# A hybrid encoder layer on one core: the head rebuilt (norm weights turned by TensorE, x split straight from PSUM, sums of squares per token, first two weight tiles worked on alternately)

## The chip, the core and the metric

The kernel runs on one core of a Trainium2 chip. The time is device microseconds for one execution; before the change the median of three runs is 1083.7 us (1081.27 to 1084.81). The engines are TensorE (PE, matmuls; its weight loads are PEld), VectorE (DVE), ScalarE (ACT), GpSimd (POOL) and SyncE (SP), which here only issues DMAs.

## The reference

One encoder layer on x of shape 1 x 512 x 1024 in float32:

```python
x = x + 0.5 * swiglu(rmsnorm(x, ffn1_norm), ffn1_w_gate, ffn1_w_up, ffn1_w_down)
h = rmsnorm(x, mix_norm); p = h @ w_in
# p -> differential attention (4 heads, relative bias) and Hyena (FFT convolution)
x = x + concat([att_out, hy_out]) @ w_out
x = x + 0.5 * swiglu(rmsnorm(x, ffn2_norm), ffn2_w_gate, ffn2_w_up, ffn2_w_down)
return rmsnorm(x, final_norm)

def rmsnorm(x, g): return x * rsqrt(mean(x * x, axis=-1) + 1e-6) * g
def swiglu(x, wg, wu, wd): return (silu(x @ wg) * (x @ wu)) @ wd
```

D_FF is 2816. The Hyena filters come from a small network of three layers on positions (33 -> 64 -> 64 -> 64, with sines), which reads only its own inputs.

## The kernel before

The activations lie transposed: eight blocks of 128 features by 512 tokens. `resid` holds x, `x_hi` and `x_lo` are the two halves (high and low part, fp32r) of x times the norm's gain, and 1/rms of each token is multiplied on afterwards (`rinv`, 128 x 512). A weight tile is 1024 x 128 numbers (512 KB). SP loads it into one of four slots of `raw`, ScalarE rounds it to `w_hi` (`split`, two buffers), VectorE subtracts to get `w_lo`, and TensorE does 24 matmuls of 128 x 512 in the routine `tile` (three for each of eight blocks: hi x hi, hi x lo, lo x hi; L1079 to L1081). The tiles have numbers in the order in which they are used, n0 to n167; the first half-step `gate_up` takes n0 to n43, four for each of 11 iterations (gate, up, gate, up).

Each engine has its own program, written out by hand, and they meet only at semaphores. SP issues in program order: the four chunks of x (L343), n0 to n3, then `others()` (25 small and middle loads, among them the four 512 KB tables `cos_t`, `sin_t`, `cos_i`, `sin_i`), and then n4 and so on. The raw slot of n4 is that of n0.

The head: TensorE turns x (`x_nat`, tokens on partitions) block by block through four PSUM banks (L1126); VectorE copies each block to `resid` (L783), ScalarE squares it (L453) and makes `x_hi` (L455), GpSimd adds the squares into `ssq` (L383), VectorE makes `x_lo` (L698). TensorE sums `ssq` over the partitions after n0 (L1090), ScalarE takes the root, VectorE inverts 128 x 512 (L703). The gain comes by a DMA that puts 1024 single numbers into columns.

The filter network's three matmuls (`mlp`, L1117) are in the iterations 0, 1 and 2 of `gate_up`, between its second and third tile; VectorE forms the sine's argument (`mlp_argument`, L715 and on) between the scaling of gate (L744) and up (L749). A matmul `vec` follows iteration 2.

Of the kernel before, what the change touches and what calls it, by code (L numbers as in the profile page):

```python
# [8 lines left out]
F32 = mybir.dt.float32  # L31
# [39 lines left out]
X_BANKS = (3, 4, 5, 6)  # L71
# [24 lines left out]
def build(nc, a, out):  # L96
    ctx = ExitStack()
    with ctx:
# [32 lines left out]
        soft, _ = place("soft", [P, 8])  # L131
        mlp_c, _ = place("mlp_c", [FO, 4])
# [46 lines left out]
        spec_q, _ = place("spec_q", [P, NT, S], at=attn_t_at)      # L179
# [7 lines left out]
        x_nat, _ = place("x_nat", [P, NT, D], at=hid_at)  # L187

# [34 lines left out]

        x_turned, resid_set, resid_sq, ssq_added, x_hi_made, x_split = (
# [58 lines left out]
        def _(sp):  # L283
# [36 lines left out]
            def gate_up(wg, wu, n_first):  # L320
# [7 lines left out]
                body(0)  # L328
                if n_first == N_FF1:
                    others()  # L330
                with sp.Fori(1, NF // 2) as i:
                    body(i)
# [9 lines left out]
            for k in range(4):  # L342
                sp.dma_start(x_nat[:, :, 2 * k * P:2 * (k + 1) * P], x[:, :, 2 * k * P:2 * (k + 1) * P]).then_inc(x_landed[k], 16)  # L343
            gate_up(a["ffn1_w_gate"][0], a["ffn1_w_up"][0], N_FF1)
# [20 lines left out]
        def _(pool):  # L365
# [9 lines left out]
            def squares(s):  # L375

                wait(pool, ssq_summed, s)
                nc.gpsimd.memset(ssq[:], 0.0).then_inc(ssq_added, 1)
                with pool.Fori(0, KD // 2) as i:
                    for b in range(2):  # L380
                        pool.wait_ge(resid_sq, number(KD * s + b + 1, 2, i))
                        pool.wait_ge(ssq_added, number((KD + 1) * s + b + 1, 2, i))
                        nc.gpsimd.tensor_tensor(ssq[:], ssq[:], sq[:, b, :], ALU.add).then_inc(ssq_added, 1)  # L383

            squares(0)

# [47 lines left out]
        def _(act):  # L434

            act.dma_start(ident[:], a["c_ident"]).then_inc(ident_landed, 16)
            with nc.allow_non_contiguous_dma(reason="columns of constants"):
                act.dma_start(cols[:, COLS["ffn1_norm"]:COLS["ffn1_norm"] + KD],
                              a["ffn1_norm"].rearrange("o (k p) -> p (o k)", p=P)).then_inc(gain_landed, 16)
# [9 lines left out]
            def resid_block(s, j, stride=0, i=0):  # L449
                at = number(j, stride, i)  # L450
                act.wait_ge(resid_set, number(KD * s + j + 1, stride, i))
                wait(act, ssq_added, number((KD + 1) * s + j, stride, i))
# [5 lines left out]
            def root(s):  # L458

                act.wait_ge(ssq_summed, s + 1)  # L460
# [7 lines left out]
            def gate_up(ffn, n_first, i, first=False, other=None):  # L468
                for b in range(2):
# [3 lines left out]
                    if not (first and b == 1):  # L473
# [3 lines left out]
                    if early:  # L477
# [5 lines left out]
                    split(8, n + (3 if early else 2), 4, i)  # L483
# [10 lines left out]

            act.wait_ge(consts_set, 4)
            act.wait_ge(gain_landed, 16)
# [958 lines left out]
```

## Time and profile before

| | |
|---|---|
| median of three runs | 1083.7 us |
| span of the profiled execution (first to last instruction) | 1079.7 us |
| time around the span (median less span) | 4.0 us |
| TensorE busy | 1042.6 us, 97% |
| VectorE busy | 576.0 us, 53% |
| ScalarE busy | 335.2 us, 31% |
| first weight matmul starts | 18.82 us |
| tile n4 starts | 46.68 us |
| mean granted TensorE clock | 0.990 |

TensorE is the engine to read: the others are busy half the time or less. A busy share near 1 says that what comes out of a faster head is kept only where TensorE isn't made to wait afterwards.

### The profile page before, as it was taken

How to read it: one execution, taken by the hardware profiler on the slowest of the kernel's cores; microseconds unless marked ns; L12 is line 12 of the kernel's file. 1: busy time of each engine (PE TensorE's matmuls, PEld its weight loads, DVE VectorE, ACT ScalarE, POOL GpSimd, SP SyncE). 2: the span in 40 equal slices, each digit the busy share in tenths (PEclk: the TensorE clock that was granted, in tenths of full speed). 3: DMA queues.
4: the chain of work that ended last, by engine and by line, in shares of the span. 5: the costliest groups of instructions: out<-in, count | busy, mean ns of one | idle time of the engine just before them, and what ended most of it. 6: DMA issues, size and time to landing. Idle time of an engine off the chain costs nothing. (4 is left out here: it accounts for less than half of the span.)

```text
span 1079.7 us, 12092 instructions
## 1 busy us (share of the span) xinstructions
PE 1042.6 (97%) x4524; PEld 818.8 (76%) x4524; DVE 576.0 (53%) x722; ACT 335.2 (31%) x475; POOL 72.4 (7%) x65
## 2 busy tenths in 40 slices
PE   5999999999999999999999969999999999999996
PEld 4776888888888875777775558778888888888885
DVE  5755545444333348876958495764444444433332
ACT  4322222222222232444444303442222323222222
POOL 4000000000000010000000070310000000000000
PEclk9999999999999999999999989999999999999999
DMA  8622333333323252323211000233333333323322
GB/s 165 197 85 80 96 97 97 97 97 92 98 83 107 88 168 81 95 59 96 78 59 59 1 20 20 78 99 97 97 97 97 97 97 93 96 88 93 91 66 78
DMA packets 185483, 96.67 MB, mean 90 GB/s; under 512 B 15843, under 2 KB 182883, under 8 KB 185448
## 3 DMA queue, kind: packets, MB, share of 16 engines
q1 hardware_dynamic: 183160, 92.70, 29.6%
q10 hardware_dynamic: 1936, 1.64, 0.5%
q0 software_dynamic: 352, 1.85, 0.5%
q8 instruction: 23, 0.38, 0.2%
q14 instruction: 12, 0.10, 0.0%
HBM read 94.07 MB, written 2.11 MB: 89 GB/s over the span
## 5 line engine op out<-in xcount | busy, mean ns | idle before, releaser
L1079 PE MATMUL bank<-x_hi,w_hi 128*128 128x512 f32 x896 | 355.3, 397 | 3.8 <-DVE w_lo L677 2.1
L1080 PE MATMUL bank<-x_lo,w_hi 128*128 128x512 f32 x896 | 349.7, 390 | 0.0
L1081 PE MATMUL bank<-x_hi,w_lo 128*128 128x512 f32 x896 | 349.6, 390 | 0.0
L677 DVE TENSOR_TENSOR w_lo<-raw,w_hi 128x1024 fp32r<-128x1024 f32 x168 | 204.6, 1218 | 225.6 <-ACT w_hi L446 219.9
L446 ACT CAST w_hi<-raw 128x1024 fp32r<-128x1024 f32 x168 | 172.2, 1025 | 166.6 <-PE bank L1081 132.5
L1079 PEld LDWEIGHTS bank<-x_hi,w_hi 128*128 128x128 f32 x896 | 168.7, 188 | 50.5 <-issue 8.6
L1080 PEld LDWEIGHTS bank<-x_lo,w_hi 128*128 128x128 f32 x896 | 168.9, 188 | 35.7 <-issue 1.4
L1081 PEld LDWEIGHTS bank<-x_hi,w_lo 128*128 128x128 f32 x896 | 168.8, 188 | 35.4
L1081 PE MATMUL bank<-h_hi,w_lo 128*128 128x512 f32 x352 | 138.7, 394 | 0.0
L1079 PE MATMUL bank<-h_hi,w_hi 128*128 128x512 f32 x352 | 138.7, 394 | 0.0
L1080 PE MATMUL bank<-h_lo,w_hi 128*128 128x512 f32 x352 | 138.7, 394 | 0.0
L383 POOL TENSOR_TENSOR ssq<-ssq,sq 128x512 f32<-128x512 f32 x32 | 43.9, 1371 | 693.9 <-ACT sq L453 693.3
L485 ACT CAST h_hi<-bank 128x512 f32 (+1 forms) x44 | 25.8, 587 | 207.7 <-DVE bank L754 207.7
L1079 PEld LDWEIGHTS bank<-h_hi,w_hi 128*128 128x128 f32 x352 | 65.8, 187 | 16.4
L1080 PEld LDWEIGHTS bank<-h_lo,w_hi 128*128 128x128 f32 x352 | 65.8, 187 | 16.3
L1081 PEld LDWEIGHTS bank<-h_hi,w_lo 128*128 128x128 f32 x352 | 65.8, 187 | 16.2
L749 DVE TENSOR_TENSOR bank<-bank,rinv 128x512 f32<-128x512 f32 x44 | 30.8, 699 | 70.5 <-PE bank L1081 70.3
L482 ACT ACTIVATE silu<-bank 128x512 f32<-128x512 f32 x44 | 26.4, 599 | 133.7 <-DVE bank L744 133.7
L744 DVE TENSOR_TENSOR bank<-bank,rinv 128x512 f32<-128x512 f32 x44 | 30.8, 699 | 39.5 <-PE bank L1081 39.4
L757 DVE TENSOR_TENSOR h_lo<-bank,h_hi 128x512 f32 (+1 forms) x44 | 30.4, 691 | 36.5 <-ACT h_hi L485 36.5
L453 ACT ACTIVATE sq<-resid 128x512 f32<-128x512 f32 (+1 forms) x32 | 20.1, 629 | 85.1 <-DVE resid L692 69.2
L698 DVE SCALAR_TENSOR_TENSOR x_lo<-resid,cols,x_hi 128x512 fp32r<-128x512 f32 (+1 forms) x24 | 31.2, 1313 | 17.8 <-ACT x_hi L455 17.7
(185 smaller groups left out, 750.2 us busy)
## 6 DMA issues: line engine op xcount, KB each, us to landing
raw<-in_ffn_w_gate SPq DMA_DIRECT2D x44, 512.0 KB, 3.8
raw<-in_ffn_w_up SPq DMA_DIRECT2D x44, 512.0 KB, 3.8
raw<-in_ffn_w_down SPq DMA_DIRECT2D x32, 512.0 KB, 3.5
raw<-in_w_in SPq DMA_DIRECT2D x24, 512.0 KB, 3.7
raw<-in_ffn_w_down SPq DMA_DIRECT2D x16, 384.0 KB, 3.1
raw<-in_w_out SPq DMA_DIRECT2D x8, 512.0 KB, 3.5
x_nat<-in_x SPq DMA_DIRECT2D x4, 512.0 KB, 6.2
out<-o_nat SPq DMA_DIRECT2D x8, 256.0 KB, 2.9
```

The lines of the kernel that those rows point to most:

```text
L383: nc.gpsimd.tensor_tensor(ssq[:], ssq[:], sq[:, b, :], ALU.add).then_inc(ssq_added, 1)
L446: nc.scalar.copy(w_hi[:, half, 0:kb, :], raw[:, slot, 0:kb, :]).then_inc(w_hi_made, 1)
L482: nc.scalar.activation(silu[:, b, :], bank[b][:], ACT.Silu).then_inc(gate_act, 1)
L485: nc.scalar.copy(h_hi[:, number(b, 2, i), :], bank[2 + b][:]).then_inc(h_hi_made, 1)
L677: nc.vector.tensor_tensor(w_lo[:, half, 0:kb, :], raw[:, slot, 0:kb, :], w_hi[:, half, 0:kb, :].bitcast(F32), ALU.subtract).then_inc(w_spl ...
L698: nc.vector.scalar_tensor_tensor(x_lo[:, at, :], resid[:, at, :], cols[:, bass.ds(at + COLS[GAIN[s]], 1)], x_hi[:, at, :].bitcast(F32), AL ...
L744: nc.vector.tensor_tensor(bank[b][:], bank[b][:], rinv[:], ALU.mult).then_inc(gate_scaled, 1)
L749: nc.vector.tensor_tensor(bank[2 + b][:], bank[2 + b][:], rinv[:], ALU.mult).then_inc(up_scaled, 1)
L757: nc.vector.tensor_tensor(h_lo[:, at, :], bank[2 + b][:], h_hi[:, at, :].bitcast(F32), ALU.subtract).then_inc(h_split, 1)
L1079: nc.tensor.matmul(dst, w_hi[:, half, k, :], hi, start=first and k == 0, stop=False)
L1080: nc.tensor.matmul(dst, w_hi[:, half, k, :], lo, start=False, stop=False)
L1081: ins = nc.tensor.matmul(dst, w_lo[:, half, k, :], hi, start=False, stop=last and k == kb - 1)
```

## The change

- SP issues n0 first, then two chunks of x, n1, two chunks of x, n2 and n3; `others()` stays ahead of n4.
- The norm's gain is loaded as eight rows of 128 and turned by a TensorE transpose; VectorE copies it to `cols`.
- TensorE begins with ten matmuls on the constant `ones`. The turned blocks of x go to six banks; `x_hi` and `x_lo` are made from the bank, with the gain. `resid` is copied beside that (two blocks by ScalarE, six by VectorE).
- n0 and n1 are worked on in pieces (`x_part`), between the turning of the chunks.
- The sum of squares comes from ScalarE, per token, on `x_nat` (four activations of 128 x 1024 with an accumulated output), the root and the reciprocal are 128 x 4, and four matmuls in the middle of n2 spread it over `bank[7]`. GpSimd has no part in it.
- The root table is loaded at the start. The iteration 0 has no `mlp`: the network's steps are in iterations 1, 2, 3.
- In the rest the counts of the semaphores are lowered by what the head no longer does; the work is the same.

The core of the diff:

```diff
+                    load(g[:, :, 0:P], KD, 0)
+                    x_chunk(0)
+                    x_chunk(1)
+                    load(u[:, :, 0:P], KD, 1)
+                    x_chunk(2)
+                    x_chunk(3)
+                    load(g[:, :, P:2 * P], KD, 2)
+                    load(u[:, :, P:2 * P], KD, 3)
                     others()
...
+            act.dma_start(gain_rows[:], a["ffn1_norm"].rearrange("o (k p) -> (o k) p", p=P)).then_inc(gain_landed, 16)
...
-            squares(0)
...
+            nc.scalar.activation(x_r[:, 12:13], eps[:], ACT.Sqrt)
+            split(8, 0)
+            act.wait_ge(gain_set, 1)
+            x_high(0)
+            x_high(1)
+            split(8, 1)
+            x_high(2)
+            x_keep(0)
+            x_high(3)
+            x_keep(1)
+            for j in range(4, KD):
+                x_high(j)
...
+            for i in range(5):
+                gate_up(0, N_FF1, i, first=i == 0, other=(lambda: mlp_sin(i - 2)) if i > 1 else None)
...
+            split(8, 0)
+            x_low(0)
+            x_low(1)
+            split(8, 1)
+            for j in range(2, KD):
+                x_low(j)
+            for j in range(KEPT_BY_ACT, KD):
+                nc.vector.tensor_copy(resid[:, j, :], bank[X_BANKS[j]][:]).then_inc(x_kept, 1)
+            for i in range(4):
+                gate_up(0, N_FF1, i, first=i == 0, other=mlp_argument(i - 1) if i else ())
...
+                    if first and ffn == 0:
+                        if b == 0:
+                            continue
+                        pe.wait_ge(x_kept, 2)
+                        tile(bank[1][:], x_ops, 2, between=x_spreads)
+                        pe.wait_ge(x_kept, 3)
+                        tile(bank[3][:], x_ops, 3)
+                        continue
...
+            for _ in range(WARM):
+                nc.tensor.matmul(bank[0][:, 0:P], ones[:], ones[:], start=True, stop=True)
             pe.wait_ge(ident_landed, 16)
...
+            x_turn(0)
+            x_turn(1)
+            pe.wait_ge(w_split, 1)
+            x_part(0, (0, 1))
+            x_turn(2)
+            pe.wait_ge(w_split, 2)
+            x_part(1, (0, 1))
+            x_part(0, (2, 3))
+            x_turn(3)
+            x_part(0, (4, 5, 6, 7))
+            x_part(1, (2, 3, 4, 5, 6, 7))
+            for i in range(4):
+                gate_up(0, N_FF1, i, first=i == 0, other=(lambda: mlp(i - 1)) if i else None)
```

SP's program from its start, before (`raw` is a tile's load, w_gate and w_up by turns, so n0 to n3):

```order
L343 DMA x_nat<-in_x 128x4x256 x4
L290 DMA raw<-in_ffn_w_gate 128x8x128
L290 DMA raw<-in_ffn_w_up 128x8x128
L290 DMA raw<-in_ffn_w_gate 128x8x128
L290 DMA raw<-in_ffn_w_up 128x8x128
L294 DMA z_t<-in_c_z 33x512
```

And in the change:

```order
L275 DMA raw<-in_ffn_w_gate 128x8x128
L338 DMA x_nat<-in_x 128x4x256 x2
L275 DMA raw<-in_ffn_w_up 128x8x128
L338 DMA x_nat<-in_x 128x4x256 x2
L275 DMA raw<-in_ffn_w_gate 128x8x128
L275 DMA raw<-in_ffn_w_up 128x8x128
L279 DMA z_t<-in_c_z 33x512
```

The tiles n0 and n1 moved between the chunks of x; what follows them, z_t and the rest of `others()`, starts at the same place.

TensorE's program around the network's first matmul, before (between n1 and n2):

```order
L1079 MATMUL bank<-x_hi,w_hi 128x512
L1080 MATMUL bank<-x_lo,w_hi 128x512
L1081 MATMUL bank<-x_hi,w_lo 128x512
L1117 MATMUL bank<-z_t,w_115 64x512 [waits mlp_landed]
L1079 MATMUL bank<-x_hi,w_hi 128x512 [waits w_split]
```

And in the change (between n5 and n6):

```order
L1130 MATMUL bank<-x_hi,w_hi 128x512
L1131 MATMUL bank<-x_lo,w_hi 128x512
L1132 MATMUL bank<-x_hi,w_lo 128x512
L1178 MATMUL bank<-z_t,w_117 64x512 [waits mlp_landed]
L1130 MATMUL bank<-x_hi,w_hi 128x512 [waits w_split,h_split]
```

The matmul on `z_t` is the same; it stands four tiles later, behind n4 and n5.

## Rows read from the trace of the kernel before

**Rows 1.** The page: span, and busy time (share) and instructions of TensorE

```profile
span 1079.7 us, 12092 instructions
...
PE 1042.6 (97%) x4524; PEld 818.8 (76%) x4524; DVE 576.0 (53%) x722; ACT 335.2 (31%) x475; POOL 72.4 (7%) x65
```

**Rows 2.** Waits of TensorE, whole span, the first: us in total, times, longest us

```profile
PE bank L1313 <- DVE spec_p L1028: 8.9, 2, 8.7
```

**Rows 3.** Timeline of SP's queue: start us, us, what it issued

```profile
10.29 1.72 SPq L290 DMA_DIRECT2D raw<-in_ffn_w_up  x1
12.05 1.28 SPq L294 DMA_DIRECT2D z_t<-in_c_z  x1
...
30.69 0.48 SPq L290 DMA_DIRECT2D raw<-in_ffn_w_gate  x1
```

**Rows 4.** DMA issues, us to landing: x (min/median/max), n3's and n4's

```profile
DMA to landing us min/median/max: 4.1/6.2/8.1
...
raw<-in_ffn_w_up SPq DMA_DIRECT2D x1, 512.0 KB, 7.3
...
raw<-in_ffn_w_gate SPq DMA_DIRECT2D x1, 512.0 KB, 10.4
```

**Rows 5.** Timeline of TensorE: first transposes, n0's matmuls; chain of work: last transposes

```profile
5.03 3.65 PE L1126 MATMUL bank<-ident,x_nat 128*128 128x128 f32 x16 [5.03 <-DMA x_nat<-in_x]
...
22.38 0.63 PE L1081 MATMUL bank<-x_hi,w_lo 128*128 128x512 f32 x1
22.81 0.63 PE L1079 MATMUL bank<-x_hi,w_hi 128*128 128x512 f32 x1
...
1067.08 3.28 PE bank L1392 x28
```

**Rows 6.** Timelines of all engines: a split into its matmul, and n4's

```profile
27.28 1.21 DVE L677 TENSOR_TENSOR w_lo<-raw,w_hi 128x1024 fp32r<-128x1024 f32 x1
...
28.64 0.19 PEld L1079 LDWEIGHTS bank<-x_hi,w_hi 128*128 128x128 f32 x1 [0.24 <-DVE w_lo L677]
...
41.24 0.39 PE L1079 MATMUL bank<-x_hi,w_hi 128*128 128x512 f32 x1
...
43.42 1.04 ACT L446 CAST w_hi<-raw 128x1024 fp32r<-128x1024 f32 x1
...
44.49 1.23 DVE L677 TENSOR_TENSOR w_lo<-raw,w_hi 128x1024 fp32r<-128x1024 f32 x1 [1.60 <-ACT w_hi L446]
...
46.68 0.39 PE L1079 MATMUL bank<-x_hi,w_hi 128*128 128x512 f32 x1
```

**Rows 7.** Timeline of TensorE around mlp(0), and at n7 and n11

```profile
34.33 0.39 PE L1081 MATMUL bank<-x_hi,w_lo 128*128 128x512 f32 x1
...
35.65 0.50 PE L1079 MATMUL bank<-x_hi,w_hi 128*128 128x512 f32 x1
...
65.67 0.50 PE L1079 MATMUL bank<-x_hi,w_hi 128*128 128x512 f32 x1 [1.27 <-DVE w_lo L677]
...
88.62 0.39 PE L1081 MATMUL bank<-x_hi,w_lo 128*128 128x512 f32 x1
89.86 0.50 PE L1079 MATMUL bank<-x_hi,w_hi 128*128 128x512 f32 x1 [0.85 <-DVE w_lo L677]
```

**Rows 8.** Stretches (busy of each engine, granted clock, DMA share, GB/s) and timeline

```profile
627.00:636.00 9.00, 0.31 (x3) 0.06 (x1) 8.86 (x8) 1.04 (x1) 8.86 (x7) 0.72 0.00 0
636.00:641.00 5.00, 5.00 (x12) 4.01 (x13) 4.96 (x8) 0.00 (x0) 0.35 (x1) 0.50 0.07 3
...
635.94 6.32 PE L1313 MATMUL bank<-cos_i,spec_p 128*128 128x256 f32 x16 [8.69 <-DVE spec_p L1028]
647.71 3.61 PE L1313 MATMUL bank<-sin_i,spec_q 128*128 128x256 f32 x16
```

**Rows 9.** Groups by line and form, 0 to 60 us: busy, mean ns of one

```profile
L698 DVE SCALAR_TENSOR_TENSOR x_lo<-resid,cols,x_hi 128x512 fp32r<-128x512 f32 x8 | 9.2, 1150 | 2.6 <-ACT x_hi L455 2.4
...
L744 DVE TENSOR_TENSOR bank<-bank,rinv 128x512 f32<-128x512 f32 x3 | 2.1, 699 | 1.0 <-PE bank L1081 0.9
```

More of the change, by code:

```diff
@@ L472, in gate_up @@
                     early = first and b == 0
-                    if not (first and b == 1):
+                    head = early and ffn == 0
+                    if not (first and b == 1) and not head:
                         split(8, n + 1, 4, i)
@@ L482, in gate_up @@
                     nc.scalar.activation(silu[:, b, :], bank[b][:], ACT.Silu).then_inc(gate_act, 1)
[L483 removed]
+                    if not head:
+                        split(8, n + (3 if early else 2), 4, i)
                     act.wait_ge(h_made, number(f0 + 1, 2, i))
@@ L737, in gate_up @@
                     early = first and b == 0
-                    if not (first and b == 1):
+                    head = early and ffn == 0
+                    if not (first and b == 1) and not head:
                         split(8, n + 1, 4, i)
-                    if early:
+                    if head:
+                        split(8, 2)
+                        x_inverse()
+                        split(8, 3)
+                        x_rinv()
+                    elif early:
                         split(8, n + 2, 4, i)
@@ L749, in gate_up @@
                     nc.vector.tensor_tensor(bank[2 + b][:], bank[2 + b][:], rinv[:], ALU.mult).then_inc(up_scaled, 1)
-                    if early:
+                    if early and not head:
                         split(8, n + 3, 4, i)
@@ L1070, in _, with tile @@
         def _(pe):
-            def tile(dst, operand, n0, stride=0, i=0, first=True, last=True, ready=None):
+            def tile(dst, operand, n0, stride=0, i=0, first=True, last=True, ready=None, between=None):
                 half = n0 % SPLIT
@@ L1128, in _, with x_turn @@
-            pe.wait_ge(consts_set, 4)
-            for i in range(3):
-                gate_up(0, N_FF1, i, first=i == 0, other=lambda: mlp(i))
+            def x_turn(k):
+                pe.wait_ge(x_landed[k], 16)
+                for j in (2 * k, 2 * k + 1):
+                    if j >= 6:
+                        pe.wait_ge(x_kept_act, j - 5)
+                        pe.wait_ge(x_split, j - 5)
+                    for t in range(NT):
+                        ins = nc.tensor.transpose(bank[X_BANKS[j]][:, t * P:(t + 1) * P], x_nat[:, t, j * P:(j + 1) * P], ident[:])
+                    ins.then_inc(x_turned, 1)
@@ new lines, in x_part @@
+            def x_part(n, ks):
+                for k in ks:
+                    pe.wait_ge(x_split, k + 1)
+                    hi, lo = x_ops[k]
+                    nc.tensor.matmul(bank[2 * n][:], w_hi[:, n, k, :], hi, start=k == 0, stop=False)
+                    nc.tensor.matmul(bank[2 * n][:], w_hi[:, n, k, :], lo, start=False, stop=False)
+                    ins = nc.tensor.matmul(bank[2 * n][:], w_lo[:, n, k, :], hi, start=False, stop=k == KD - 1)
+                if ks[-1] == KD - 1:
+                    ins.then_inc(w_used, 1)
@@ new lines, in x_spreads @@
+            def x_spreads():
+                pe.wait_ge(x_inv, 1)
+                pe.wait_ge(x_kept, 4)
+                for t in range(NT):
+                    ins = nc.tensor.matmul(bank[7][:, t * P:(t + 1) * P], x_r[:, 8 + t:9 + t].to_broadcast([P, P]), ident[:],
+                                           start=True, stop=True)
+                ins.then_inc(x_spread, 1)
+            pe.wait_ge(consts_set, 1)
+            for _ in range(WARM):
+                nc.tensor.matmul(bank[0][:, 0:P], ones[:], ones[:], start=True, stop=True)
```

122 lines of the change are left out of this document (72 added, 50 removed).

## The prediction

> **What bounds the kernel now.** I read the page's share of busy time first, then the waits of TensorE, then the timelines of the first 50 us and the single DMA issues. TensorE is busy 97% of the span [rows 1]. Of its waits over the whole execution [rows 2] the largest is 8.9 us before the inverse transform, which the change doesn't touch; at the head it waits for x until 5.03 [rows 5] and then within the turning of x. From the first weight tile on, TensorE runs tile after tile: 24 matmuls of 512 columns, from 41.24 to 46.68, are 5.44 us [rows 6], 0.227 us each. So whatever the head wins is kept only if TensorE is fed without a pause up to the point where both kernels do the same again. The tiles are numbered n0, n1, ... in the order of their weights. n0 to n3 have their raw slots free from the start; n4 is the first whose load stands in SP's program behind the small loads of `others()`, in both kernels. I take **the start of tile n4** as the common point: 46.68 us before [rows 6].
>
> SP issues the last early tile (n3) at 10.29, begins `others()` at 12.05, which ends with the tables `cos_t`, `sin_t`, `cos_i`, `sin_i` (512 KB each), and issues n4's load only at 30.69 [rows 3]. That load lands 10.4 us later [rows 4], at 41.1, since 2 MB of tables are ahead of it in the same queue. ScalarE rounds it at 43.42, VectorE makes the low part at 44.49 [rows 6]. Before, n4 thus landed 2.3 us before it was rounded: the load was covered, but barely.
>
> **The change, part by part.**
>
> *The head on TensorE, if nothing else limited it.* The DMA order becomes n0, x chunks 0 and 1, n1, x chunks 2 and 3, n2, n3. Before, x landed from 4.9 us on, chunk 3 at 10.5 (4.1 and 8.1 us after issues at 0.75 and 2.4), n3 at 17.6 [rows 3, 4]: 7.1 us for four tiles of weights, 1.8 each, and at the rate of the first chunks 1.5 to 1.8 for one of x. Laid out anew: n0 5.3, x0 6.9, x1 8.4, n1 10.3, x2 11.8, x3 13.3, n2 15.1, n3 16.9. Sixteen transposes take 3.65 us at the start and 28 take 3.28 us at the end of the kernel [rows 5]. Turning chunks 0 and 1 fills 6.9 to 10.6 at the slower pace. Then come 48 matmuls of n0 and n1 and 16 transposes: 48 x 0.227 + 16 x 0.117 = 12.8 us, and some 0.6 us for what still runs at the low clock: n1 ends near 24.0. ScalarE and VectorE keep up. Their steps are about 0.7 us for each block (a multiply on VectorE out of a bank and `rinv` has mean 0.70 [rows 9]), and the two squares on either side of n2's rounding stand behind no matmul: 1.2 us each, a little over the 1.04 us of a rounding of 1024 elements [rows 6]. The six copies of x to `resid` on VectorE (0.61 us apart) end at 22.6, n2's low part at 23.8, just before it is wanted. n2 and n3 take 10.9 us, the spreading of 1/rms 0.9 (four fp32 matmuls on 128 columns: between four passes of 0.117 and eight of 0.228, so 0.5 to 1.8). **TensorE finishes n3 near 35.8**, 10.9 us before it did. Taken off the path on the way: eight squares and additions (ScalarE, GpSimd), a root table load, a reciprocal of 128x512. I price them at nothing by themselves, since their gain is in the 35.8. The ten matmuls on `ones` and the turning of the norm's rows stand before x lands (20 passes of 0.228 are 4.6 us, from 1 us on), and cost nothing. `x_lo` is now made from a bank: 0.70 by the nearest bank operand, 1.15 by its own mean beside a busy GpSimd [rows 9]; eight times the difference is 3.6 us and would put n3's end at 39.4. Should the clock rise only at 15.6 instead of about 12, n3 ends at 37.6; with the low clock until 23 us, as before, at some 41.3. The start of n4 below doesn't depend on it.
>
> *What n4 waits for.* n4's load still follows `others()`. The gains of the head move SP only through its back-pressure: the issue of n3 took until 12.0 as I read it because the queue was full [rows 3]. With the column load of `ffn1_norm` (1024 elements of 4 bytes) gone and n0's packets first, I put the end of that issue at 11.0, and z_t's, held 1.3 us before, 0.5 to 1 us earlier than it was. From there to 30.69 SP is paced by its own issues, 0.4 to 0.6 us each, which are the same. So n4 lands 0 to 1.3 us earlier; I take 0.8: 40.3. From landing to the first matmul: 0.15 for the hop (x landed at 4.85, the first transpose began at 5.03 [rows 5]), 1.08 from rounding to the low part, 1.21 to its end and 0.15 to the weight load (27.28 + 1.21 = 28.49, load at 28.64) [rows 6]. Sum 2.6: **n4 starts at 42.9**, against 46.68: 3.8 us won, and TensorE stands idle for 7.1 us, from 35.8 on. Of the 10.9 us, 7.1 are lost there.
>
> *The filter network moves by one iteration.* `mlp(0)` ran on TensorE in iteration 0, ahead of n4; now it follows n5. Its price there: from the start of the last matmul, 34.33, to the next tile's first, 35.65, is 1.32 instead of 0.23, so 1.09 us [rows 7]. That is owed after n4, and is subtracted. Besides, each of the iterations 1 and 2 before has a wait for `w_lo` at its fourth tile, since VectorE's up-scaling stands behind the wait for the network's matmul, then `h`, `h_hi` and ScalarE's next rounding behind it: idle 1.27 at 65.67 and 0.85 at 89.86 [rows 7], with the lost pace 1.4 and 1.0 us (88.62 to 89.86 is 1.24 instead of 0.23). Iteration 0 had none; now iterations 1, 2 and 3 have one each. One more: 1.0 to 1.4, I take 1.2.
>
> *The clock after the idle stretch.* The one long pause before, 8.7 us up to 635.94, shows what follows: over 627 to 636 the granted clock averages 0.72, so it fell from 2.4 to 1.2 GHz within the pause; over 636 to 641 it is 0.50, and 16 matmuls took 6.32 us that later took 3.61 [rows 8]: 2.7 us. Pauses of 1.3 us and less cost nothing of the kind [rows 7]. Bounds 0 and 2.7; at 7.1 us I take 2.7, since that is nearer to 8.7 than to 1.3.
>
> The Trainium skill (TensorE: Matmul & The Clock Gate, section HAM oscillation — how this bites in real kernels) speaks against this change in the same way: matmuls that wait for DMA come back at half rate, and the cost of getting the clock back is paid at each such wait. By the rule the 2.7 us stand; if only the short pauses were a guide, the sum would be 2.7 us lower.
>
> *Sum*, against the profiled execution, whose span is 1079.7 [rows 1] and which with 4.0 us around it stands at the median of 1083.7: -3.8 (n4's start) + 1.1 (`mlp(0)`) + 1.2 (one more wait) + 2.7 (clock) = **+1.2 us: 1084.9**. What comes after (projections, attention, transforms, second half) has the same instructions in the same order, and is not moved against itself. GpSimd's additions at the head went alongside VectorE and are gone; nobody on the path feels it after n4.
>
> **The rivals.**
>
> *A: as summed*, 1084.9. Own range 1083.5 to 1086.5 (landing 0 to 1.3, wait 1.0 to 1.4, clock price 2.0 to 2.7).
>
> *B: n4 waits, but the clock stays at 2.4 GHz.* If the head is slower than 35.8 (late clock, late x), the pause gets short while n4's start stays at 42.9; the pauses of 1.3 us left it up [rows 7]. 1083.7 - 1.5 = 1082.2. For: several estimates in the head lean to the optimistic side. Against: it needs 3 us more.
>
> *C: faster, since the pause is much shorter than I make it.* If SP got through `others()` some 2.7 us earlier (DMA queue freer, small issues at 0.43 us throughout instead of 0.6), n4 would start at 41.0 and with the clock up the gain is 3.3 us, the point from which it counts. Were n4's load not held up at all, n4 would start with the end of n3 and the result would be 10.8 - 2.3 = 8.5 us faster, 1075.2. Against: n4's 10.4 us from issue to landing [rows 4] and the unchanged list in front of it.
>
> The Trainium skill (DMA: Bandwidth & Descriptors, section Anatomy of one DMA — SWDGE (gpsimd) path) gives a DMA a fixed 2.0 us and then its bytes at 436 GB/s; for n4's 512 KB that is an estimate of 3.2 us, which would mean this case in full, but the formula has no queue in it, and the 10.4 us measured decide against it.
>
> *D: slower.* The low clock lasts through the whole of n4, not through some 5 us of it: 24 matmuls at 0.43 (22.38 to 22.81 [rows 5]) instead of 0.227 are 4.9 us instead of 2.7, giving 1087.1. It decides from a price of 4.8 us. For: the low stretch of 18.8 to 23.2 and that of 636 were each about 5 us. Against: just that; none lasted 10.
>
> That the two first tiles aren't really alternated, or that the head is slower than before, changes nothing as long as n3 ends before 42.9.
>
> **How the numbers follow.** A 0.50, B 0.25, C 0.13, D 0.12. A measurement of this kernel can tell about 0.3% (3.3 us) from no change. A and B are within it, C is faster, D slower by more than it: but A's and B's edges and the spread of the runs (1081.3 to 1084.8) can carry a little over. Faster 0.14, same 0.75, slower 0.11. The range takes in A and B with that spread and reaches into C and D: 1080.6 to 1087.3.
>
> **What would show it right or wrong.** Right: TensorE's first weight matmul before 12 us, n3's last near 36; then a pause of 5 to 8 us that ends with `w_lo` of n4, SP's issue of n4 still near 30 us, its landing about 10 us later; a granted clock near 0.5 in the 5 us behind the pause; three waits for `w_lo` of 0.8 to 1.3 us in iterations 1, 2, 3. Wrong: n4's load landing before 38 (C); n3 ending after 39 (B); or a difference from the kernel before that arises after the first 110 us, which no step here accounts for.

## The result, and the profile after

The changed kernel takes 1074.21 us (median of 5 runs, 1071.75 to 1077.74), the kernel before in the same comparison 1083.15 us (5 runs, 1078.41 to 1084.81). The ratio on record is 0.994 (it is not the quotient of the two medians, which would be 0.992), with a 95% interval of 0.9912 to 0.9967: faster by 3.6 to 9.5 us. The forecast was 1084.9, with a range of 1080.6 to 1087.3, so it missed on both counts: the time lies below the range, and "same" had 0.75 of the chance.

The page of the changed kernel, its span and the busy times, to be read beside [rows 1]:

```profile
span 1075.9 us, 12082 instructions
...
PE 1040.3 (97%) x4551; PEld 824.4 (77%) x4551; DVE 568.8 (53%) x722; ACT 335.0 (31%) x477; POOL 60.9 (6%) x57
```

Its profiled execution took 1077.74 us, the slowest of its five. The span is 3.8 us shorter than before. The waits of TensorE, the first two (us in total, times, longest us), beside [rows 2]:

```profile
PE bank L1130 <- DVE w_lo L707: 12.0, 5, 9.0
PE bank L1410 <- DVE spec_p L1079: 9.2, 2, 8.7
```

A new wait for `w_lo` of 9.0 us has come in: the pause ahead of tile n4. TensorE's timeline at the head (start us, us, what it did, in brackets the idle time before and what ended it), with ScalarE's and VectorE's step for n4 in between:

```profile
10.07 0.48 PE L1195 MATMUL bank<-x_hi,w_hi 128*128 128x512 f32 x1
...
23.17 0.39 PE L1130 MATMUL bank<-x_hi,w_hi 128*128 128x512 f32 x1
...
34.30 0.39 PE L1130 MATMUL bank<-x_hi,w_hi 128*128 128x512 f32 x1
...
41.70 1.04 ACT L440 CAST w_hi<-raw 128x1024 fp32r<-128x1024 f32 x1 [8.62 <-DMA raw<-in_ffn_w_gate]
42.77 1.22 DVE L707 TENSOR_TENSOR w_lo<-raw,w_hi 128x1024 fp32r<-128x1024 f32 x1 [10.33 <-ACT w_hi L440]
44.14 0.76 PE L1130 MATMUL bank<-x_hi,w_hi 128*128 128x512 f32 x1 [9.00 <-DVE w_lo L707]
```

The first weight matmul runs at 10.07, n2 starts at 23.17, n3 is through at 34.98 (three matmuls after 34.30), and n4, which before started at 46.68 [rows 6], starts at 44.14. SP's queue and the landing of n4, beside [rows 3, 4]:

```profile
10.19 2.82 SPq L279 DMA_DIRECT2D z_t<-in_c_z  x1
...
19.08 2.56 SPq L290 DMA_DIRECT2D cols<-in_hy_bias  x1
...
32.26 0.62 SPq L275 DMA_DIRECT2D raw<-in_ffn_w_gate  x1
```

```profile
raw<-in_ffn_w_gate SPq DMA_DIRECT2D x1, 512.0 KB, 9.4
```

n4 is issued at 32.26 and lands 9.4 us later, at 41.7. What the pause does to the clock shows in three stretches (busy time of TensorE, its weight loads, VectorE, ScalarE and GpSimd, then the granted clock, the DMA share and GB/s):

```profile
34.50:44.00 9.50, 0.64 (x3) 0.19 (x1) 1.23 (x2) 1.04 (x1) 0.00 (x0) 0.64 1.14 333
44.00:47.40 3.40, 3.26 (x8) 2.61 (x9) 2.39 (x4) 1.53 (x2) 0.00 (x0) 0.50 1.15 287
47.40:60.00 12.60, 12.60 (x54) 9.48 (x53) 4.68 (x6) 1.53 (x2) 0.00 (x0) 1.00 0.31 89
```

The clock fell within the pause from 2.4 to 1.2 GHz (mean 0.64), stayed there for the 3.40 us after it, and was back at 1.00.

**Where the two traces part.** A good clock along the kernel is the start of each tile's `w_lo` on VectorE, since all 168 tiles have one. The starts for n20, n44 and n68, first before, then after:

```profile
138.04 1.23 DVE L677 TENSOR_TENSOR w_lo<-raw,w_hi 128x1024 fp32r<-128x1024 f32 x1 [1.60 <-ACT w_hi L446]
268.60 1.23 DVE L677 TENSOR_TENSOR w_lo<-raw,w_hi 128x1024 fp32r<-128x1024 f32 x1 [1.60 <-ACT w_hi L446]
391.82 1.23 DVE L677 TENSOR_TENSOR w_lo<-raw,w_hi 128x1024 fp32r<-128x1024 f32 x1 [4.85 <-ACT w_hi L446]
```

```profile
139.27 1.23 DVE L707 TENSOR_TENSOR w_lo<-raw,w_hi 128x1024 fp32r<-128x1024 f32 x1 [1.60 <-ACT w_hi L440]
269.83 1.23 DVE L707 TENSOR_TENSOR w_lo<-raw,w_hi 128x1024 fp32r<-128x1024 f32 x1 [1.60 <-ACT w_hi L440]
389.65 1.23 DVE L707 TENSOR_TENSOR w_lo<-raw,w_hi 128x1024 fp32r<-128x1024 f32 x1 [4.69 <-ACT w_hi L440]
```

At n20, behind the head and all that it disturbs, the changed kernel is 1.23 us *behind*. At n44 it is still exactly 1.23 behind: the gate and up tiles run at one pace in both. From n44 to n68, the down projection of the first feed-forward block, it gains 3.40 us (+1.23 to -2.17), and in the same stage of the second block (n144 at 939.86, n167 at 1054.01, against 940.07 and 1057.45) another 3.23. The head, which the change is about, gave nothing; stages whose instructions the change doesn't touch gave the time.

### The profile page after: what moved, and what is told of

Its sections match the earlier page's. It is cut to its first block and busy times, and to the rows that moved or that the text cites. A ratio compares the mean times of both kernels' runs of the same rounds, so it can differ in the third digit from the quotient of the medians.

```text
span 1075.9 us, 12082 instructions
## 1 busy us (share of the span) xinstructions
PE 1040.3 (97%) x4551; PEld 824.4 (77%) x4551; DVE 568.8 (53%) x722; ACT 335.0 (31%) x477; POOL 60.9 (6%) x57
## 5 line engine op out<-in xcount | busy, mean ns | idle before, releaser
L1130 PE MATMUL bank<-x_hi,w_hi 128*128 128x512 f32 x880 | 349.4, 397 | 12.4 <-DVE w_lo L707 12.0
L1131 PE MATMUL bank<-x_lo,w_hi 128*128 128x512 f32 x880 | 344.1, 391 | 0.0
L1132 PE MATMUL bank<-x_hi,w_lo 128*128 128x512 f32 x880 | 344.1, 391 | 0.0
L1130 PEld LDWEIGHTS bank<-x_hi,w_hi 128*128 128x128 f32 x880 | 166.2, 189 | 59.9 <-issue 18.8
L1132 PEld LDWEIGHTS bank<-x_hi,w_lo 128*128 128x128 f32 x880 | 166.1, 189 | 35.3
L1131 PEld LDWEIGHTS bank<-x_lo,w_hi 128*128 128x128 f32 x880 | 166.4, 189 | 34.5 <-issue 1.0
L380 POOL TENSOR_TENSOR ssq<-ssq,sq 128x512 f32<-128x512 f32 x24 | 32.5, 1353 | 651.1 <-ACT sq L447 650.8
L447 ACT ACTIVATE sq<-resid 128x512 f32<-128x512 f32 (+1 forms) x24 | 15.1, 630 | 78.2 <-DVE resid L722 67.0
L804 DVE TENSOR_TENSOR bank<-bank,silu 128x512 f32<-128x512 f32 x44 | 30.8, 700 | 4.5
```

The lines of the kernel that those rows point to most:

```text
L804: nc.vector.tensor_tensor(bank[2 + b][:], bank[2 + b][:], silu[:, b, :], ALU.mult).then_inc(h_made, 1)
L1130: nc.tensor.matmul(dst, w_hi[:, half, k, :], hi, start=first and k == 0, stop=False)
L1131: nc.tensor.matmul(dst, w_hi[:, half, k, :], lo, start=False, stop=False)
L1132: ins = nc.tensor.matmul(dst, w_lo[:, half, k, :], hi, start=False, stop=last and k == kb - 1)
```

## The experiments

**Reading the pace of the matmuls.** In the down projection the moving operand is `h_hi` or `h_lo` instead of `x_hi` or `x_lo`; everything else is as in the gate and up tiles. Four starts of TensorE in a row, before and then after:

```profile
330.34 0.39 PE L1079 MATMUL bank<-h_hi,w_hi 128*128 128x512 f32 x1
330.58 0.39 PE L1080 MATMUL bank<-h_lo,w_hi 128*128 128x512 f32 x1
330.81 0.39 PE L1081 MATMUL bank<-h_hi,w_lo 128*128 128x512 f32 x1
331.04 0.39 PE L1079 MATMUL bank<-h_hi,w_hi 128*128 128x512 f32 x1
```

```profile
330.57 0.39 PE L1130 MATMUL bank<-h_hi,w_hi 128*128 128x512 f32 x1
330.80 0.39 PE L1131 MATMUL bank<-h_lo,w_hi 128*128 128x512 f32 x1
331.03 0.39 PE L1132 MATMUL bank<-h_hi,w_lo 128*128 128x512 f32 x1
331.25 0.39 PE L1130 MATMUL bank<-h_hi,w_hi 128*128 128x512 f32 x1
```

From the first to the fourth it is 0.70 us before and 0.68 after, so one matmul is 0.2333 us before and 0.2267 after. The whole stage bears it out: between the starts of `w_lo` of n44 and n68, with 528 matmuls, lie 123.22 us before and 119.82 after, 0.2334 and 0.2269 each. The mean duration that the profile gives moves with it and is easier to look up: 394 ns before, 389 after. The groups by line and form, before and after:

```profile
L1079 PE MATMUL bank<-h_hi,w_hi 128*128 128x512 f32 x352 | 138.7, 394 | 0.0
```

```profile
L1130 PE MATMUL bank<-h_hi,w_hi 128*128 128x512 f32 x352 | 136.9, 389 | 0.0
```

There are 3 x 352 = 1056 such matmuls, so 1056 x 0.0066 = 7.0 us (an estimate; the starts above give 3.40 us for the one stage and 3.23 for the other up to its last tile); the 96 of the output projection whose moving operand is `mh_hi` or `mh_lo` are sped up too (n100 to n104: 0.63 us).

What differs is an address. The tiles are placed one behind the other in a partition of SBUF, and the change puts `x_r` ([P, 16], 64 bytes) ahead of `mlp_c`. Everything placed after it, `h_hi` and `h_lo` among it, lies 64 bytes later: `h_hi` at byte 138560 before, at 138624 after. `x_hi` (32896) and `w_hi` (82048) stay. **Theory:** these 64 bytes are the whole gain, the head gives about +0.1%. **Rival:** the new head brings the gain in some way that shows only later.

**before_h_moved: the 64 bytes alone, with the old head.**

```diff
         soft, _ = place("soft", [P, 8])
+        _, _ = place("pad", [P, 16])
         mlp_c, _ = place("mlp_c", [FO, 4])
```

> The kernel before, with 64 unused bytes placed ahead of mlp_c, where the change puts x_r: h_hi, h_lo and everything that lies behind start 64 bytes later, on a multiple of 128. Theory (the place of the moving operand sets the pace of its matmuls): in the two down stages (24 tiles each) the pace goes from 0.233 us to 0.227 us a matmul, 3.3 us won in each, some 0.8 us more in the output projection, 7 us in all: about 0.9935 of before. Rival (the pace in the down stages comes from the new head, its clock or its queues): no difference, 1.000, and the means of the h matmuls stay at 394 ns.

Measured: 1072.59 us against 1081.39, ratio 0.9928 (0.9909 to 0.9946), and the h matmuls have a mean of 389 ns:

```profile
L1080 PE MATMUL bank<-h_hi,w_hi 128*128 128x512 f32 x352 | 136.9, 389 | 0.0
```

A tile that nobody uses makes the old kernel as fast as the changed one.

**after_h_back: the new head alone**, with `x_r` placed behind `h_lo`.

```diff
-        x_r, _ = place("x_r", [P, 16])
         mlp_c, _ = place("mlp_c", [FO, 4])
...
         h_lo, _ = place("h_lo", [P, NF, S], F32R)
+        x_r, _ = place("x_r", [P, 16])
```

> The changed kernel, with x_r placed behind h_lo, so that h lies where it lay before. Theory: the down stages are back at 394 ns, and what is left is the head alone: 1.2 us slower than before (1.001), against the changed kernel 7 us slower. Rival (the head itself makes the gain): stays at 0.994 of before.

Measured: 1082.49 us (12 runs) against 1081.39, ratio 1.0011 (0.9995 to 1.0027), with the old pace:

```profile
L1130 PE MATMUL bank<-h_hi,w_hi 128*128 128x512 f32 x352 | 138.7, 394 | 0.0
```

The two runs together decide for the theory: the gain comes with the 64 bytes and goes with them, whichever head the kernel has. Its trace is also a second look at the same head:

```profile
42.20 0.77 PE L1130 MATMUL bank<-x_hi,w_hi 128*128 128x512 f32 x1 [7.14 <-DVE w_lo L707]
```

n4 starts 1.94 us earlier than in the changed kernel's trace, behind a pause of 7.1 us instead of 9.0, and at n20 and n44 this kernel is 0.07 us ahead of before, not 1.23 behind. So the net of the head differs by 1.3 us between two executions of the same head.

**What about the address counts?** Seen from w, x is at a distance of 0 and h of 192 bytes modulo 256 before; after, h is at 0 too. Three questions were open: whose address counts, moving, stationary or the distance between the two; modulo what; and whether the x matmuls can be slowed the same way.

**before_x_moved: x moved by 64 bytes, w and h by 128**, so that h stays where it was seen from w and x doesn't.

```diff
+        _, _ = place("pad_a", [P, 16])
         resid, _ = place("resid", [P, KD, S])
...
+        _, _ = place("pad_b", [P, 16])
         raw, _ = place("raw", [P, RAW, 8, P])
```

> The kernel before, with 64 unused bytes ahead of resid and 64 more ahead of raw: resid, x_hi and x_lo lie 64 bytes off a multiple of 128, the weights and h lie to a multiple of 128 bytes as they did (h stays 64 off). Theory (a moving operand that starts off a multiple of 128 bytes is read at 0.2333 us for 512 columns, not at 0.2267): the 2688 matmuls on x lose 0.0066 us each, 17.7 us: 1.016 of before, and the means of the x matmuls go from 390 to 394 ns or more. Rival (something peculiar to h, such as its place at the end of the memory): no difference.

Measured: 1093.93 us against 1081.14, ratio 1.0109 (1.0084 to 1.0133). The x matmuls became slow, by the 0.0066 us each that h had been slow before (n20 to n44, 24 tiles of 24 matmuls, 3.84 us longer); h is slow still:

```profile
L1082 PE MATMUL bank<-x_lo,w_hi 128*128 128x512 f32 x896 | 354.8, 396 | 0.0
...
L1081 PE MATMUL bank<-h_hi,w_hi 128*128 128x512 f32 x352 | 139.2, 396 | 0.0
```

The 12.8 us fall short of the 17.7 that all 2688 x matmuls come to. The starts of `w_lo` beside those of before say where: n4 to n20 loses 2.33 us, n20 to n44 3.84 and n104 to n144 6.67, each within 0.4 us of what the matmuls there come to. The 24 tiles of the attention and hyena projections, n68 to n92, lose 1.96 instead of 3.8, so part was covered by TensorE's waits for others. Between n92 and n96 1.80 us come back, and that is not the matmuls but the clock: over 580 to 600 us it was granted at 0.91 in the trace of before and at 1.00 in this one.

**before_w_moved: w moved by 64 bytes against x, h by 64 against w.** It tells a rule of the moving operand's own address from one of the distance.

```diff
+        _, _ = place("pad_a", [P, 16])
         raw, _ = place("raw", [P, RAW, 8, P])
...
+        _, _ = place("pad_b", [P, 16])
         mlp_c, _ = place("mlp_c", [FO, 4])
```

> The kernel before, with 64 unused bytes ahead of raw and 64 ahead of mlp_c: the weights (raw, w_hi, w_lo) and the constants behind them start 64 bytes later, x and h lie to a multiple of 128 as they did. Theory (only the moving operand counts; weight loads have slack beside the matmuls): no difference, 1.000, means 390 (x) and 394 ns (h). Rival (the stationary operand counts as well): all weight matmuls lose, 0.0066 us for each of 3744, 25 us.

Measured: 1088.36 us, ratio 1.0061 (1.0042 to 1.0081). Neither expectation held. The x matmuls are slow though x hasn't moved, and the h matmuls are fast:

```profile
L1082 PE MATMUL bank<-x_lo,w_hi 128*128 128x512 f32 x896 | 355.0, 396 | 0.0
...
L1081 PE MATMUL bank<-h_hi,w_hi 128*128 128x512 f32 x352 | 136.9, 389 | 0.0
```

What fits both lines, and all runs above, is the distance: x to w is now 192 modulo 256, h to w is 0. The time fits too: 12.8 us for slow x, as in before_x_moved, less 7.6 for fast h is 5.2, and 7.2 were measured (4.5 to 8.8).

**before_all_at_64: all three operands moved off their old residues, with all distances at 0.** It tells the distance from a rule of the two addresses each by itself.

```diff
+        _, _ = place("pad_a", [P, 16])
         resid, _ = place("resid", [P, KD, S])
...
+        _, _ = place("pad_b", [P, 16])
         mlp_c, _ = place("mlp_c", [FO, 4])
```

> The kernel before, with 64 unused bytes ahead of resid (everything moves) and 64 more ahead of mlp_c (h moves twice): x, the weights and h all start 64 bytes off a multiple of 128. Theory (only the distance of the moving operand from the stationary one counts, modulo 128 bytes): x stays at 390 ns and h goes to 389, 7 us faster than before, 0.9935. Rival (each operand for itself must start on a multiple of 128): x at 396, h at 396, some 18 us slower, 1.017.

Measured: 1072.21 us against 1081.56, ratio 0.9913 (0.9887 to 0.994); both kinds are fast:

```profile
L1082 PE MATMUL bank<-x_lo,w_hi 128*128 128x512 f32 x896 | 350.4, 391 | 0.0
...
L1081 PE MATMUL bank<-h_hi,w_hi 128*128 128x512 f32 x352 | 136.9, 389 | 0.0
```

So the distance counts, not the place: at 192 modulo 256 each, the three do as well as at 128.

**before_h_by_32 and before_h_by_192: two more distances for h**, 224 and 128 (192 + 32 and 192 + 192, modulo 256).

```diff
         soft, _ = place("soft", [P, 8])
+        _, _ = place("pad", [P, 8])
         mlp_c, _ = place("mlp_c", [FO, 4])
```

> The kernel before, with 32 unused bytes ahead of mlp_c: h starts 96 bytes off a multiple of 128 instead of 64. Theory A (any start off a multiple of 128 costs the same): no difference, 394 ns. Theory B (64-byte units: a start that is no multiple of 64 is worse still): the h matmuls above 394 ns, 3 us or more slower. Theory C (only the distance 64 is bad): 389 ns, 7 us faster.

Measured: 1080.18 us (10 runs), ratio 0.9994 (0.998 to 1.0008).

```diff
         soft, _ = place("soft", [P, 8])
+        _, _ = place("pad", [P, 48])
         mlp_c, _ = place("mlp_c", [FO, 4])
```

> The kernel before, with 192 unused bytes ahead of mlp_c: h starts on a multiple of 256, the weights 128 off one. Theory (the distance counts modulo 128): h at 389 ns, 7 us faster, 0.9935. Rival (it counts modulo 256; all fast pairs so far had the same place modulo 256 as well): h stays at 394 to 396 ns, 1.000.

Measured: 1080.73 us (10 runs), ratio 0.9994 (0.9977 to 1.0011). Both leave h slow, first 32 bytes, then 192:

```profile
L1080 PE MATMUL bank<-h_hi,w_hi 128*128 128x512 f32 x352 | 139.2, 396 | 0.0
```

```profile
L1080 PE MATMUL bank<-h_hi,w_hi 128*128 128x512 f32 x352 | 139.0, 395 | 0.0
```

With 128 slow, a period of 128 bytes falls, which I had thought the likelier; 256 holds. A period of 512 is out too: after the change h lies 256 modulo 512 from w and is fast. Distances of 32, 64, 96 and 160 were not run. In one table (distance of the moving from the stationary operand modulo 256, mean ns):

| kernel | x to w | x_lo | h to w | h_hi |
|---|---|---|---|---|
| before | 0 | 390 | 192 | 394 |
| after, before_h_moved | 0 | 391, 390 | 0 | 389 |
| after_h_back | 0 | 391 | 192 | 394 |
| before_x_moved | 192 | 396 | 192 | 396 |
| before_w_moved | 192 | 396 | 0 | 389 |
| before_all_at_64 | 0 | 391 | 0 | 389 |
| before_h_by_32 | 0 | 390 | 224 | 396 |
| before_h_by_192 | 0 | 391 | 128 | 395 |

The means of the slow ones differ by up to 2 ns, but their pace doesn't: from n44 to n68 it takes 123.22 us in before, after_h_back, before_h_by_32 and before_h_by_192 (123.38 in before_x_moved), and 119.82 in after, before_h_moved and before_all_at_64 (120.00 in before_w_moved).

One more rival would be that the matmuls are held up by what other engines read and write, since whatever is moved against `w_hi` is moved against `raw` as well. The traces speak against it: in the down projection, from 270 to 385 us, the steps from one matmul to the next during which VectorE and ScalarE are both idle (197 before, 199 after) have a mean of 0.233 us before and 0.227 after, as the others have. DMA traffic was not looked at in this way.

**The head: what the 11 us were lost to.** after_h_back showed that the new head by itself gives +0.1%. By the prediction's own reading n3 ends early but n4's load stands behind the four tables in SP's queue. **Theory:** take the load from behind the tables and the gain of the head comes through. **Rival:** the pause only moves to the next tile whose load is late.

**after_n4_first: n4's and n5's loads ahead of `others()`,** n6's and n7's right behind it.

```diff
+                    load(g[:, :, 2 * P:3 * P], KD, 4)
+                    load(u[:, :, 2 * P:3 * P], KD, 5)
                     others()
+                    load(g[:, :, 3 * P:4 * P], KD, 6)
+                    load(u[:, :, 3 * P:4 * P], KD, 7)
                 else:
                     body(0)
-                with sp.Fori(1, NF // 2) as i:
+                with sp.Fori(2 if n_first == N_FF1 else 1, NF // 2) as i:
```

> The changed kernel, with the loads of n4 and n5 issued ahead of the 25 loads of others(), the rest as it was. Theory (n4 waits in SP's queue only): the 9.0 us pause before n4 is gone, n4 starts near 35, right behind n3, and the clock stays at 2.4 GHz; others() and n6 move 2 to 3 us later, which may leave 1 to 2 us of waiting at n6. Against the changed kernel 9.2 + 1.6 less up to 2 = 9 to 11 us faster, 0.985 of before. Rival (the pause moves to n6 whole, since the tables are still ahead of it): n6 starts only near 50, and 5 us or less are won.

Measured: 1066.01 us against 1081.39, ratio 0.9869 (0.9848 to 0.9891). TensorE goes on to n4 with almost no pause:

```profile
35.97 0.47 PE L1134 MATMUL bank<-x_hi,w_hi 128*128 128x512 f32 x1 [0.27 <-DVE w_lo L711]
```

All its waits for `w_lo` come to 2.9 us, the longest 0.9: the pause didn't move to n6. At n44 this kernel is 9.74 us ahead of the changed one (260.09 against 269.83).

**after_tables_late: only the four tables moved**, behind n11's load; n4's load keeps its place behind the small loads.

```diff
-                with sp.Fori(1, NF // 2) as i:
+                first = 1
+                if n_first == N_FF1:
+                    for i in (1, 2):
+                        for b in range(2):
+                            load(g[:, :, (i * 2 + b) * P:(i * 2 + b + 1) * P], KD, 4 * i + 2 * b)
+                            load(u[:, :, (i * 2 + b) * P:(i * 2 + b + 1) * P], KD, 4 * i + 2 * b + 1)
+                    tables()
+                    first = 3
+                with sp.Fori(first, NF // 2) as i:
```

> The changed kernel, with the tables moved in the same way and nothing else: n4 stays behind the small loads of others(). Theory (of the wait for n4 the larger part is the tables' issues, 2 us, and their transfer, 6 to 7 us): n4 is issued near 29, lands 4 us later and starts at 35 to 36; the pause shrinks from 9.0 to under 1.5 us and the clock stays up: 9 to 10.5 us faster than the changed kernel, 0.985 of before. Rival (SP's small issues are what n4 waits for): the pause stays over 4 us, 5 us or less are won.

Measured: 1068.75 us (4 runs) against 1081.56, ratio 0.9879 (0.984 to 0.9917). SP issues n4 at 28.40, and n4's first matmul is there 6.91 us later:

```profile
28.40 0.42 SPq L275 DMA_DIRECT2D raw<-in_ffn_w_gate  x1
```

```profile
35.31 0.47 PE L1140 MATMUL bank<-x_hi,w_hi 128*128 128x512 f32 x1 [0.27 <-DVE w_lo L717]
```

The tables were what n4 waited for: with 2 MB of them ahead in the queue the landing alone took 9.4 us, here 4.3. The small loads of `others()` no longer hold up TensorE, whose wait ahead of n4 is 0.27 us.

**before_tables_late: the same move in the old kernel.**

```diff
+                    tables()
+                    first = 3
+                with sp.Fori(first, NF // 2) as i:
```

(with the loads of n4 to n11 ahead of it, as in the diff above)

> The kernel before, with the four tables (2 MB) issued behind the load of n11 instead of ahead of n4's. Theory (in the old head n4's load was covered, since it landed 2.3 us before it was rounded): n4 still starts at 46.7, no difference, 1.000. Rival (the tables' transfers cost the old head something as well): faster by 2 us or more.

Measured: 1080.85 us (10 runs), ratio 0.9995 (0.998 to 1.001). The old head ended late enough to hide n4's load, so moving the tables was worth nothing there: in the trace the start of `w_lo` of n4 is 0.37 us later than before, as that of n0 already was. The two edits are worth something only together: the head alone +0.1%, the tables alone 0, both (with h at its new place) 1.2%, of which 7.6 us, 0.7%, are h's.

**after_filled: the pause filled with matmuls**, to price the clock. Behind tile n3, 36 matmuls of `x_hi` by `x_hi` into a free bank are added; nobody reads them.

```diff
                         tile(bank[3][:], x_ops, 3)
+                        pe.wait_ge(x_kept, 6)
+                        for _ in range(36):
+                            nc.tensor.matmul(bank[4][:], x_hi[:, 0, 0:P], x_hi[:, 1, :], start=True, stop=True)
```

> The changed kernel, with 36 matmuls of 512 columns (x_hi by itself, into bank 4, which nobody reads) behind n3: 8.2 us of work in the 9.0 us pause, as a measure of what the low clock after the pause costs. Theory: the clock stays at 2.4 GHz through n4, n4 takes 5.46 us instead of 7.1, and the end is 1.6 us earlier than that of the changed kernel. Rival (the first matmuls of n4 are slow for another reason, the cold start of the tile): no difference.

Measured: 1074.25 us, ratio to before 0.9945 (0.9923 to 0.9967), no difference from the changed kernel's 1074.21, so the medians leave the price open. The trace gives it:

```profile
34.94 8.32 PE L1158 MATMUL bank<-x_hi 128*128 128x512 f32 x36
43.10 0.39 PE L1130 MATMUL bank<-x_hi,w_hi 128*128 128x512 f32 x1
...
48.54 0.39 PE L1130 MATMUL bank<-x_hi,w_hi 128*128 128x512 f32 x1
```

Tile n4 now takes 43.10 to 48.54, 5.44 us, with the granted clock at 1.00. In the changed kernel it took 7.11 (44.14 to 51.25). The pause of 9.0 us thus costs 1.67 us through the clock. The filler overran: `w_lo` of n4 started at 39.84 and took 1.23 in this run, so it was ready at 41.07, 2.0 us before the filler ended, which is more than what the clock gave back.

**best: all of it together.** after_n4_first, with the tables behind n15's load, and the filter network's matmul ahead of the up tile, so that VectorE has its result before it is asked for the next `w_lo`.

```diff
+            def tables():
                 sp.dma_start(cos_t[:], a["c_cos"].rearrange("(t p) f -> p t f", p=P)).then_inc(dft_landed, 16)
...
+                    for i in (2, 3):
...
+                    tables()
...
-                    tile(bank[2 + b][:], x_ops, n + 1, 4, i)
                     if other and b == 0:
                         other()
+                    tile(bank[2 + b][:], x_ops, n + 1, 4, i)
```

> The changed kernel with n4 and n5 ahead of others(), the four tables (2 MB) behind the load of n15, and the network's matmul on TensorE ahead of the up tile instead of behind it. Against after_n4_first: the wait for w_lo in the fourth tile of iterations 1, 2, 3 (0.8 to 1.3 us idle each) should go, since VectorE finds the network's sum ready when it comes to it: 3 us faster, some 1063 us, 0.984 of before. Rival (VectorE's argument steps delay the next low part all the same): 1066, no difference.

Measured: 1063.15 us (1060.8 to 1064.2) against 1081.14, ratio 0.9827 (0.9806 to 0.9848): 1.7% faster than the kernel before, and 11 us below the changed one. The largest wait of TensorE is now the old one before the inverse transform:

```profile
PE bank L1421 <- DVE spec_p L1090: 8.8, 1, 8.8
```

The waits for `w_lo`, 12.0 us in the changed kernel and 2.9 in after_n4_first, are down to one of 0.3 us, ahead of n4:

```profile
PE bank L1141 <- DVE w_lo L718: 0.3, 1, 0.3
```

These 2.6 us are most of the 2.9 that lie between the medians of after_n4_first and this run. The move of the tables and that of the network's matmul were not run apart.

## Why the prediction was wrong

**What bounds the kernel: right.** TensorE is busy 97% of the span in both, and its waits tell the head's story.

**The head: right in the mechanism, and in the net only by luck as close as it looks.** Measured is the place at n20 and n44: 1.23 us behind before; predicted was +1.2. In after_h_back, the same head, it is 0.07 us ahead of before, and the five other kernels with the old head and fast x matmuls lie between 1.54 us ahead of before's trace and 0.35 behind it at n20. The 0.03 us between +1.2 and +1.23 are chance, and errors cancelled in it. Term by term (the third column is after_h_back):

| step | predicted | changed kernel | same head again |
|---|---|---|---|
| n1 ends | 24.0 | 23.2 | 23.1 |
| n3 ends | 35.8 | 34.98 | 34.9 |
| n4's load lands | 40.3 | 41.7 | 39.7 |
| n4 starts | 42.9 | 44.14 | 42.20 |
| won by n4's start | 3.8 | 2.54 | 4.48 |
| pause ahead of n4 | 7.1 | 9.0 | 7.1 |
| the clock after it | 2.7 | 1.67 | 2.34 |
| wait at n7, shorter (0.92 for 1.27) | 0 | -0.35 | -0.34 |
| `mlp(0)` and one more wait | 2.3 | 2.44 | 2.41 |
| sum | +1.2 | +1.23 | -0.07 |

(The last two terms are read from the starts of `w_lo` beside those of before: the changed kernel is 0.87 us ahead at n6, 1.22 ahead from n8 to n12, and 1.23 behind at n20. Between n12 and n20 lies iteration 3, in which it alone has a network's matmul and a wait.) The two terms that were mis-sized are n4's landing and the clock.

*The landing.* (`others()` has 28 loads by the code, not 25, in both kernels.) I had n4's issue come 0.8 us earlier than 30.69; it came 1.57 later. The end of n3's issue did move, to 10.14 (11.0 predicted), but z_t's then took 2.82 us instead of 1.28 and ended at 13.01 against 13.33, so of the early end 0.3 us were left. That is so in after_filled and after_h_back as well (2.46 and 2.75 us). Besides, one of the small column loads (`in_hy_bias`, at 19.08) took 2.56 where its neighbours take 0.5 to 0.6; in the other two it took 0.81 and 0.99, and n4 was issued at 30.54 in after_filled and at 31.08 in after_h_back. So this term has a spread of 1.7 us from one execution to another, which a single trace of before can't show, and for which my 0 to 1.3 had no room on the late side.

*The clock.* I took the 2.7 us from the pause before the inverse transform [rows 8] as the nearest row. The size of the pause didn't decide it: 9.0 us cost 1.67, 8.7 us cost 2.7 [rows 8], and 7.1 us in after_h_back cost 2.34. What decided was how long the low clock lasted after it: 3.40 us, some 5 and 4.40. The Trainium skill (TensorE: Matmul & The Clock Gate, section HAM oscillation — how this bites in real kernels) counts the penalty as the throttled time times (1 - 1.2/2.4), half of it. The traces agree: 3.40 us at 0.50 make 1.7, and 1.67 were measured; 4.40 make 2.2, and 2.34 were measured.

Rival A is therefore what the head does; B, C and D are out for the head: the clock did fall, n4 did not come early, and the low clock ended before the tile did. after_h_back, the change without the move of h, measured 1082.49 against 1081.39, 1.1 us more (by the interval -0.5 to +2.9), and is where the prediction's +1.2 us would have been right. The measured 1074.21 lies close to the 1075.2 that C names for a load that isn't held up at all; that is chance, since here it was held up for 9 us. And A's own range is mis-added at its upper end: 1084.9 + 0.8 (no earlier landing) + 0.2 (a wait of 1.4) is 1085.9, not 1086.5.

**The step that failed** is one sentence: "What comes after (projections, attention, transforms, second half) has the same instructions in the same order, and is not moved against itself." The instructions and their order are the same. Their operands are not in the same place: h lay 64 bytes further on, and 1056 matmuls of it, with 96 of the output projection, ran at 0.2267 us instead of 0.2333, 7.6 us together. The diff shows the line that does it, `x_r`'s `place`; I read it as a small tile and not as a shift of all that is placed behind it. The trace of before held the other half of the hint: x_lo's group of matmuls had a mean of 390 ns and h_hi's, of the same form, 394. I took no notice of a difference of 1% between groups that should be alike. The sign that the prediction named for this, a difference that arises after the first 110 us, is the one that appeared.

**The base was off too.** I put 4.0 us around the span, taking the profiled execution for the median one. In every other run the time lies 1.8 to 3.3 us above the span. Neither the 4.0 us of the execution of 1083.7 nor the 1.6 of that of 1081.27 is among these, so which execution of before was traced isn't shown. That the base was high is: the medians of before were 1081.39, 1081.14 and 1081.56 in the later comparisons; 1081.4 + 1.2 - 7.6 = 1075.0, against 1074.21 measured.

**What stays open.** The profiled execution of the changed kernel loses 2.54 us between n68 and n72 against before. A stretch there, in the hyena and attention projections, has the low clock:

```profile
412.00:419.00 7.00, 7.00 (x16) 4.36 (x15) 6.72 (x12) 0.26 (x1) 0.00 (x0) 0.55 0.00 0
```

TensorE was busy all through it, and the clock was low all the same. What it did just before and as the clock fell were 16 matmuls on 64 partitions (404.95 to 413.9, with one wait of 0.73 us); the same 16 left the clock at 1.00 in the trace of before. Of the 14 traces, only before, before_x_moved, before_h_by_32 and after_n4_first have a granted clock of 1.00 all the way from 395 to 430. It goes neither with the head nor with the pads, and what brings it on in one execution and not in another wasn't found. A second such place is 580 to 600 us: the clock was granted at 0.91 in before and after, at 1.00 in before_h_moved and before_x_moved, and at 0.83 in after_h_back and before_all_at_64, and by it the latter four traces shift by 1.5 to 1.9 us against before's. Two single traces can thus be compared stage by stage, but not by their spans.

The pads need no gain beyond their matmuls. By the medians before_h_moved is 8.8 us faster, by the ratio 7.8 (interval 5.8 to 9.8), and before_all_at_64 9.4 (6.5 to 12.2); both intervals hold the 7.6. And why 256 bytes of distance matter was not looked into; the runs show that they do.

## What to carry to other kernels

When memory is laid out by hand, a new tile moves every tile behind it: compare the addresses of before and after, not only the instructions, and compare the mean time of matmul groups that should be alike, since 6.6 ns on 1056 of them were worth more here than a rebuilt head. A head that feeds TensorE 11 us sooner is worth what the next load allows: follow the queue behind the last early tile (here 2 MB of tables, the first of which is not read before 575 us) before counting the gain, and move that first. An edit that measures as nothing (the tables in the old kernel) may be the one that a later edit needs.

## What the runs showed of the hardware

A matmul of 512 columns with fp32r operands takes 0.2267 us when the moving and the stationary operand are 0 modulo 256 bytes apart in the partition, and 0.2333 when they are 128, 192 or 224 apart, 2.9% more. Neither address by itself was seen to matter: with x, w and h all at 192 modulo 256 instead of 128, and their distances at 0, all are fast (before_all_at_64).

The Trainium skill (SBUF — State Buffer, section A bandwidth-pool intuition that's wrong (but worth ruling out)) gives TensorE's weight loads a second, independent read port, by which where the one operand lies should not matter to the reading of the other. The runs here speak against full independence, by those 2.9%; no run shows which of the two is held up, or that it is the port that holds it up.

A DMA of 512 KB landed 9.4 us after its issue behind 2 MB in the same queue, and 4.3 us after it with the tables gone from there (after_tables_late); its tile's first matmul, after landing, rounding and low part, then began 6.91 us after the issue.

The granted clock fell from 2.4 to 1.2 GHz within pauses of TensorE of 7.1, 8.7 and 9.0 us, and the time lost by it was 2.34, 2.7 and 1.67 us: it doesn't grow with the pause.
